# Down products and output projections on half banks of 256 columns

## The reference

```
m = mixer(rms_norm(h)) ; h = h + rms_norm(m @ w_out)
f = (silu(gate) * val) @ w_down          # gate, val from rms_norm(h) @ w_up, 2816 wide
h = h + rms_norm(f)
```

## Time and profile before

| | |
|---|---|
| median of three runs | 1214.59 us |
| profiled execution | 1215.68 us |
| its span, first to last instruction | 1213.9 us |
| mean granted TensorE clock | 0.998 |
| TensorE busy (matmul) | 1180.3 us, 97% |
| weight loads busy | 1079.3 us, 89% |
| VectorE, ScalarE, GpSimd busy | 847.2, 651.3, 149.0 us |
| DMA | 196.68 MB, mean 162 GB/s |

### The profile page before, as it was taken

How to read it: one execution, slowest core, us unless ns; L and a number is a source line. 1 busy time by engine, 2 the same in 40 slices (tenths; PEclk the granted TensorE clock), 3 DMA queues, 4 the chain that set the end, 5 groups by cost and what they waited for, 6 DMA issues and landing times.

```text
span 1213.9 us, 23231 instructions
## 1 busy us (share of the span) xinstructions
PE 1180.3 (97%) x9876; PEld 1079.3 (89%) x9876; DVE 847.2 (70%) x1299; ACT 651.3 (54%) x1171; POOL 149.0 (12%) x143
## 2 busy tenths in 40 slices
PE   8999999999999999999999999999999999999998
PEld 8887779999879898977999988899989877999986
DVE  6578867888557888886788875857577776655542
ACT  4557646666445666644666663565434534644431
POOL 1220000000002333100000000103443411000000
PEclk9999999999999999999999999999999999999999
DMA  8842135665634443353655664442232322755540
GB/s 304 266 140 88 62 103 218 209 204 183 238 106 148 177 182 141 113 175 112 243 187 197 208 242 156 176 174 105 94 118 71 111 100 87 279 181 198 182 169 35
DMA packets 31623, 196.68 MB, mean 162 GB/s; under 512 B 4000, under 2 KB 5664, under 8 KB 9376
## 3 DMA queue, kind: packets, MB, share of 16 engines
q1 hardware_dynamic: 27504, 185.17, 43.0%
q10 hardware_dynamic: 4016, 10.03, 2.6%
HBM read 193.09 MB, written 1.05 MB: 160 GB/s over the span
## 4 chain that ended last, share of the span: by engine, by line
PE 86%; DVE 6%; ACT 3%; issue 2%; POOL 1%; DMA 1%; ACTq 0%; DVEq 0%; POOLq 0%; SPq 0%
PE bank L514 24%; PE bank L516 23%; PE bank L515 23%; DVE wlo L502 2%; PE bank L1860 1%; ACT whi L495 1%; PE bank L1097 1%; PE bank L1154 1%; PE bank L1181 1%; DMA raw<-in_wall 1%; DVE xT L704 1%; PE bank L2506 1%; PE bank L688 1%; PE bank L2972 1%; PE bank L2449 1%
## 5 line engine op out<-in xcount | busy, mean ns | idle before, releaser
L502 DVE TENSOR_TENSOR wlo<-raw,whi 128x1024 fp32r<-128x1024 f32 (+1 forms) x325 | 390.0, 1237 | 92.8 <-ACT whi L495 92.1
L514 PE MATMUL bank<-xT,wlo 128*128 128x256 f32 x1544 | 434.4, 281 | 6.2 <-DVE xc L1566 2.1
L516 PE MATMUL bank<-xT,whi 128*128 128x256 f32 x1544 | 428.6, 278 | 0.0
L515 PE MATMUL bank<-xT,whi 128*128 128x256 f32 x1544 | 428.6, 278 | 0.0
L495 ACT ACTIVATE whi<-raw 128x1024 fp32r<-128x1024 f32 (+1 forms) x349 | 349.5, 1048 | 115.8 <-PE bank L516 82.8
L514 PEld LDWEIGHTS bank<-xT,wlo 128*128 128x128 f32 x1544 | 288.6, 187 | 10.6 <-issue 3.9
L515 PEld LDWEIGHTS bank<-xT,whi 128*128 128x128 f32 x1544 | 288.8, 187 | 0.9 <-issue 0.5
L516 PEld LDWEIGHTS bank<-xT,whi 128*128 128x128 f32 x1544 | 288.5, 187 | 0.2
L633 POOL TENSOR_TENSOR rr<-rr,nhalf 128x1 f32<-128x1 f32 x34 | 24.8, 729 | 714.4 <-DVE rr L621 526.7
L514 PE MATMUL bank<-whi,xT 128*128 128x256 f32 (+1 forms) x352 | 104.6, 297 | 6.6 <-DVE xT L704 6.6
L514 PE MATMUL bank<-whi,gT 128*128 128x512 f32 x264 | 104.4, 396 | 0.0
(11 more groups left out here) (369 smaller groups left out, 1654.1 us busy)
## 6 DMA issues: line engine op xcount, KB each, us to landing
raw<-in_wall SPq DMA_DIRECT2D x173, 1024.0 KB, 4.9
grow<-in_rows ACTq DMA_DIRECT2D x13, 512.0 KB, 5.6
h<-in_x SPq DMA_DIRECT2D x4, 256.0 KB, 5.6
dsk<-in_rows ACTq DMA_DIRECT2D x4, 256.0 KB, 3.5
memx<-in_mem ACTq DMA_DIRECT2D x1, 1024.0 KB, 9.9
out<-h SPq DMA_DIRECT2D x4, 256.0 KB, 2.1
masks<-in_masks SPq DMA_DIRECT2D x1, 580.0 KB, 12.6
D<-Tx ACTq DMA_DIRECT2D x4, 128.0 KB, 6.0
```

What stands on the lines that cost most here:

```text
L502: e.tensor_tensor(wlo[i % NHL][:, o:o + w], raw[i % NRAW][:, o:o + w], whi[i % NHL][:, o:o + w], SUB).then_inc(*up("dve.low", p))
L514: e.matmul(out, a[1], b[0], start=start, stop=False)
L515: e.matmul(out, a[0], b[1], start=False, stop=False)
L516: return e.matmul(out, a[0], b[0], start=False, stop=stop)
```

## The change

`pe_down` splits each matmul of 512 columns into two of 256, onto the two halves of the bank, except the three products that open a bank (start set), which stay 512 wide. The three products of the first half (columns 0 to 255) come before the three of the second half. The signals stay on the last matmul of each bank.

```diff
@@ pe_down @@
             for n in range(2):
                 for kk in range(2):
                     k = ks[kk]
-                    d = pe_three(e, banks[base + n][:, :], [a[:, k, 128 * t:128 * t + 128] for a in src],
-                                 [v[:, kk, 512 * n:512 * n + 512] for v in w], start and kk == 0, stop and kk == 1)
+                    a = [x[:, k, 128 * t:128 * t + 128] for x in src]
+                    if start and kk == 0:
+
+                        pe_three(e, banks[base + n][:, :], a, [v[:, kk, 512 * n:512 * n + 512] for v in w], True, False)
+                        continue
+                    for o in (0, 256):
+                        d = pe_three(e, banks[base + n][:, o:o + 256], a,
+                                     [v[:, kk, 512 * n + o:512 * n + o + 256] for v in w], False, stop and kk == 1 and o > 0)
                 if stop and t and n == 0:
                     d.then_inc(*up("pe.early", i))
             d.then_inc(*(up("pe.proj", i) if t else up("pe.proj", i, "first")))
```

## The result

The change made the kernel slower: median 1222.12 us of ten runs (1219.53 to 1226.53) against 1215.55 us of ten runs before (1211.85 to 1219.58), ratio 1.0051 with a 95% interval of 1.0035 to 1.0067. The forecast was 5.6 us faster.

The account below looks back on a forecast made before the run. The prediction took TensorE's rate of matmul starts as the bound. It summed -4.8 us for dense down stages and -0.8 us for interleaved ones to -5.6 us, forecasting 1209.5 us, range 1203 to 1221.

Parts of the forecast that it names:

- The bound: Whole kernel: time follows the rate at which TensorE starts the split product's matmuls, with 86% of the span on TensorE.
- The counts: pe_down's 1224 matmuls: 72 bank-opening ones stay whole, 1152 are cut, 756 in dense down stages and 396 in interleaved ones.
- The price of a cut: Two 256-column steps less one 512-column step of 233.2 ns: -6.4 ns in the fast rhythm, +2.2 ns in the slow rhythm.
- the fast rhythm: 256-column matmuls starting 113.4 ns apart, as in the up stages; assumed for dense down stages, worth -4.8 us.
- The interleaved stages: 396 cuts in the mixers' output projections, priced midway between the fast rhythm and the slow rhythm: -0.8 us.
- the upper bound of +2.2 ns: Highest price foreseen for one cut, 2 x 117.7 - 233.2 ns, from the stretch at 500.53 to 511.48 us.
- a further rhythm: Half-bank stream with a third step, a gap between 113 and 118 ns; the prediction said this would show it wrong.
- The seam at 171 us: 512-column down stream followed at once by 256-column products, stepping 113.9 ns; taken as just what a down stage does.
- Rival 2: Cut streams fall into the slow rhythm after opening products and interruptions: +2.2 ns a cut, +2.5 us, 1217.1 us; chance 0.25.
- the slow rhythm: 256-column matmuls starting 117.7 ns apart, seen at 500.53 to 511.48 us; makes a cut cost +2.2 ns.
- Rival 3: Up stages behind down products turn slow, +3.9 us each; all three with Rival 2 give 1228.8 us; chance 0.06.
- The rule of the Trainium skill: Isolated matmul stream steps N / 2.4 + 2.5 ns, so 1152 cuts cost +2.9 us; given 0.05 of Rival 2's 0.25.

Follow-up runs that it names:

- e4: Changed kernel with gT 448, 64 and 4032 bytes higher in the three feed-forward parts, yT 192, yG 960; first dense down stage 61.97 us, 117.8 ns a step.
- e5: Changed kernel with only the raw buffers at SBUF's upper end, so all TensorE reads lies 24 KB lower; down stages 62.48, 64.23 and 62.48 us.
- e14: Changed kernel with three of four bank openings 512 wide in each dense down stage, gT, yT, yG not shifted; stage 62.50 us.
- e15: Changed kernel with gT and yG 448, yT 192 bytes higher, three of four bank openings 512 wide in dense down stages; ratio 1.0005 to the kernel before.
- e17: Changed kernel with gT and yG 448, yT 192 bytes higher, two bank openings 512 wide per dense down stage; first up stage's last 912 products 103.33 us.
- e3: Changed kernel with the weight buffers raw, whi and wlo at the upper end of SBUF; 1235.74 us, ratio 1.0165 to the kernel before.
- e11: Changed kernel with gT, yT, yG 64 bytes higher and three of four bank openings 512 wide in dense down stages; ratio 1.0002 to the kernel before.
- e13: Changed kernel with gT, yT, yG 64 bytes higher and one bank opening 512 wide in each dense down stage; ratio 1.0014 to the kernel before.
- e16: Changed kernel with gT and yG 448, yT 192 bytes higher, one bank opening 512 wide per dense down stage; first up stage's last 912 products 107.38 us.
- e18: As e15, but the three mixers' output projections stay 512 wide as in the kernel before; median 1215.98 us, ratio 0.9990 to the kernel before.
- e3b: Kernel before, without the cut, with raw, whi and wlo at the upper end of SBUF; 1229.93 us, ratio 1.0126 to the kernel before.
- e7: As e3b, but with a 352-byte gap at the upper end of SBUF, so the weights lie lower; 1213.98 us in its one run.

## Why the prediction was wrong

**The bound** was right: TensorE's rate of starts sets the time, supply stays ahead, the clock stays at 2.4 GHz, and weight loads cost nothing of their own. The counts were right (1152 cuts, 72 whole).

**The price of a cut** is the step that failed: "so I take the fast rhythm for the dense stages: 756 x -6.4 ns = -4.8 us". In its place the runs show 2 x 118.7 - 233.2 = +4.2 ns, and 756 x 4.2 = +3.2 us (+3.5 by the three stages). The interleaved stages, put at -0.8 us, measured +0.87 + 0.78 - 0.19 = +1.5. So -5.6 became +4.9. Even the upper bound of +2.2 ns was too low. It came from rows with xT as the loaded operand, and I took them for "the same operands". The kernel before had rows with another buffer loaded, and I passed them by:

```profile
85.23 0.28 PE L515 MATMUL bank<-wlo,X 128*128 128x256 f32 x1
85.35 0.28 PE L516 MATMUL bank<-whi,X 128*128 128x256 f32 x1
...
88.89 0.28 PE L516 MATMUL bank<-whi,X 128*128 128x256 f32 x1
89.02 0.28 PE L514 MATMUL bank<-whi,X 128*128 128x256 f32 x1
```

From 85.23 to 89.02 us, 32 steps of 118.4 ns on average, with X loaded, and uneven: 113 to 123 ns. These were the rows that spoke for a further rhythm, the sign that the prediction itself had named as the one that would refute it.

**The seam at 171 us**, on which the choice rested, was true of xT: layer 1's cut projection, the one that loads xT, has calls of 2.72 us in place of 2.80 (that its stretch is 0.19 us shorter is no more than untouched stretches differ by). It was no evidence for gT, for two reasons that the runs separate. gT lay at an offset at which neither regular rhythm comes up (e4, e5, e14). And where it does, the number of wide groups decides, and four is an even number (e15 to e17). Nor is it what a down stage does: a down stage comes out of an up stage, by an exchange of the operands' roles that the seam doesn't have.

**Rival 2** (a cut stream in the slow rhythm, +2.5 us, chance 0.25) had the right sign and place, but not the rhythm: its 117.7 ns came up in none of the three dense stages, and its price was too small. **Rival 3**, the spread to the up stages, isn't in the profiled execution of the changed kernel, but does occur: 6 of the 48 up stages in the 16 traces without the offset of e3 run slow, in e11, e13 (two), e15, e16 and e17, 5.65 us a chunk in place of 5.44, about +4 us a stage. All six are in kernels with a shifted gT, 6 of their 24 up stages against 0 of 24 in the others; whether the shift favours them or it is chance at the entry isn't settled, nor how much of the scatter of the runs it makes.

**The rule of the Trainium skill** that spoke against the change ("TensorE: Matmul & The Clock Gate", section Back-to-back issue gap), by which each isolated matmul costs 2.5 ns over its columns, gave +2.9 us, nearer to the result than my sum. That is luck, as the traces don't bear out its reason: a fixed cost for each matmul would show in every placement, and in e15 and e18 the same 256-column products on half banks step at 113.3 ns, 6.6 ns a pair under 512 columns.

## What to carry to other kernels

In this kernel a dense stream of 256-column products has a few steps it can lock into, up to 5% apart, and which one it gets depends on where the loaded and the streamed tile begin within 512 bytes and on what stood before it. So take the step from rows with the very same two buffers, and where there are none, take the worst step that any buffer shows. Before a tile shape is judged by one per cent, try the same shape with the tiles moved by some tens to hundreds of bytes.

## What the runs showed of the hardware that I had not expected

- Offsets of tiles within 512 bytes change the step of 256-column fp32r matmuls between 113.3, 117.8, 118.3 and 118.7 ns, and leave 512 columns at 233 ns: 352 bytes take an up chunk from 5.68 to 5.44 us (e3b, e7), while the 512-column stage takes 61.36 and 61.37 us. A move by 24 KB at equal offsets changes nothing (e5).
- The even rhythms of 113.3 and 117.8 ns survive chunk borders and hundreds of products. A group of three 512-column products turns one into the other (fourteen of fourteen dense stages at a shift of 448 or 4032 bytes). At a shift of 64 bytes no group did so in the dense stages. Which offsets allow which step, and why, stays open.
- So does an exchange of the operands' roles without a gap. Over the 16 traces without the offset of e3, and with 256-column products on both sides, the change from streaming xT to loading it turned fast into slow in 33 of 33 cases and slow into fast in 13 of 17; the change back kept the rhythm in all 32. Why four stayed slow isn't known.
- An up stage can come out at either step with nothing changed ahead of it. e15, e16 and e17 issue the same instructions up to the end of the first up stage, and its last 912 products took 103.33 us in e15 and e17 and 107.38 in e16.
